# Two feed-forward layers computed as seven block products, with hidden activations passed through DRAM

## The reference

```python
D_MODEL = 1024
D_FF = -(-8 * D_MODEL // (3 * 256)) * 256
def swiglu(xn, w_gate, w_up, w_down):
    h = jax.nn.silu(jnp.einsum('bsd,df->bsf', xn, w_gate)) * jnp.einsum('bsd,df->bsf', xn, w_up)
    return jnp.einsum('bsf,fd->bsd', h, w_down)
...
        hp = hp + swiglu(rms_norm(hp, ln_ffn[layer]), w_gate[layer], w_up[layer], w_down[layer])
        hs = hs + swiglu(rms_norm(hs, ln_ffn[layer]), w_gate[layer], w_up[layer], w_down[layer])
```

## Time and profile before

| | us |
|---|---|
| median of 3 runs | 2554.5 |
| lowest, highest | 2551.43, 2556.82 |
| span of the profiled execution | 2554.3 |
| first feed-forward layer, 889.00 to 1679.65 | 790.65 |
| pooling mixer and the norm behind it, 1679.65 to 1749.30 | 69.65 |
| second feed-forward layer, 1749.30 to 2542.40 | 793.10 |
| tail | 11.90 |

### The profile page before, as it was taken

The page is one execution under the profiler, slowest core; times in us unless marked ns, Lnnn a source line. Parts: engine busy times, 40 slices in busy tenths (PEclk is TensorE's granted clock), DMA queues, the critical chain, the costliest instruction groups (busy, mean ns, idle before and its releaser), DMA issues.

```text
span 2554.3 us, 39454 instructions
## 1 busy us (share of the span) xinstructions
PE 2465.1 (97%) x16305; PEld 2288.4 (90%) x16305; DVE 1059.7 (41%) x2210; ACT 673.8 (26%) x1186; POOL 196.5 (8%) x239
## 2 busy tenths in 40 slices
PE   7999988888889999999999999999999999999998
PEld 6778866555669999999999999999999999999998
DVE  4312056555774633333223333467333333333325
ACT  5221133355673321111101111164201111111112
POOL 0020000045432000000000000040000000000000
PEclk9999999999999999999999999998999999999999
DMA  4321289944562011111011111111111111111101
GB/s 165 111 94 59 114 316 409 364 158 156 181 196 71 17 50 50 50 50 47 20 50 43 40 50 50 35 47 34 50 50 42 42 50 50 50 50 50 34 26 71
DMA packets 119688, 229.42 MB, mean 90 GB/s; under 512 B 6260, under 2 KB 82373, under 8 KB 116972
## 3 DMA queue, kind: packets, MB, share of 16 engines
q1 hardware_dynamic: 113731, 179.60, 20.3%
q0 software_dynamic: 5808, 47.64, 5.4%
HBM read 209.32 MB, written 51.41 MB: 102 GB/s over the span
## 4 chain that ended last, share of the span: by engine, by line
PE 87%; issue 4%; DMA 3%; DVE 3%; SPq 2%; ACT 1%; POOL 1%; DVEq 0%; ACTq 0%
PE ps L1834 74%; PE ps L1868 2%; PE ps L793 2%; DMA kraw<-cache_win_k_a 2%; PE ps L777 2%; PE ps L812 2%; SPq L905 1%; PE ps L1923 1%; DMA wraw<-w_out 1%; PE ps L2151 1%; ACT sm L681 1%; POOL sm L1066 1%; PE ps L1962 1%; SPq L908 0%; PE ps L1937 0%
## 5 line engine op out<-in xcount | busy, mean ns | idle before, releaser
L1834 PE MATMUL ps<-xn,ws 128*128 128x384 f32 (+1 forms) x6744 | 1117.8, 326 | 0.0
L1834 PEld LDWEIGHTS ps<-xn,ws 128*128 128x128 f32 x6744 | 1112.1, 188 | 0.8
L1834 PE MATMUL ps<-hh,ws 128*128 128x384 f32 (+1 forms) x3168 | 530.5, 327 | 0.0
L1834 PEld LDWEIGHTS ps<-hh,ws 128*128 128x128 f32 x3168 | 524.8, 188 | 0.0
L1655 DVE TENSOR_TENSOR act_h<-act_s,ps 128x384 f32<-128x384 f32 x132 | 70.2, 532 | 847.2 <-ACT act_s L1264 847.2
L1264 ACT ACTIVATE act_s<-ps 128x384 f32<-128x384 f32 x132 | 62.5, 473 | 1205.2 <-PE ps L1834 1096.5
L1634 DVE TENSOR_TENSOR x<-ps,x 128x384 f32<-128x384 f32 (+1 forms) x552 | 284.5, 532 | 187.2 <-PE ps L1834 185.4
L1834 PE MATMUL ps<-wp,xn 128*128 128x512 f32 (+1 forms) x1080 | 245.4, 389 | 0.0
L1834 PEld LDWEIGHTS ps<-wp,xn 128*128 128x128 f32 (+1 forms) x1080 | 196.3, 182 | 48.9
L622 DVE TENSOR_TENSOR ws<-wraw,ws 128x2048 fp32r<-128x2048 f32 x63 | 143.8, 2282 | 5.2 <-ACT ws L617 5.2
L1066 POOL TENSOR_TENSOR sm<-sm,pstat 128x128 f32<-128x128 f32 (+7 forms) x96 | 108.7, 1145 | 320.0 <-DVE pstat L554 320.0
(11 more groups left out here) (213 smaller groups left out, 1793.4 us busy)
## 6 DMA issues: line engine op xcount, KB each, us to landing
wraw<-w_gate SPq DMA_DIRECT2D x22, 1024.0 KB, 5.2
wraw<-w_up SPq DMA_DIRECT2D x22, 1024.0 KB, 5.2
wraw<-w_down SPq DMA_DIRECT2D x22, 1024.0 KB, 4.9
kraw<-cache_win_k_a SPq DMA_DIRECT2D x8, 2048.0 KB, 14.7
vraw<-cache_win_v_a SPq DMA_DIRECT2D x8, 2048.0 KB, 11.4
kraw<-cache_k_b SPq DMA_DIRECT2D x64, 256.0 KB, 5.8
vraw<-cache_v_b SPq DMA_DIRECT2D x64, 256.0 KB, 11.5
o_wk_s<-cache_win_k_a POOLq DMA_DIRECT2D x8, 2032.0 KB, 9.6
```

Source lines behind the costliest of these rows:

```text
L1834: r = mm(out, w(a), m(b_), start=(i == 0 and q_ == 0), stop=(i == n - 1 and q_ == 2))
```

## The change

A product of matrices cut into 2 by 2 blocks needs seven block products in place of eight when sums and differences of blocks are multiplied. The changed kernel does this for gate, up and down.

- **Units.** A unit is seven products (`PARTS`) of 272 columns (`BL`, four blocks of tokens, two to a unit: `tp`). 44 units compute gate and up (hidden block, then gate for both `tp`, then up for both), each 7 times 4 times 3 = 84 matmuls. The down product comes after them in pieces (`PIECES`): four pieces of 2 hidden blocks, each 8 units (four groups of output features by two `tp`) of 42 matmuls, and one piece of 3 blocks, 8 units of 63. That is 3696 + 1344 + 504 = 5544 matmuls a layer. Products 4, 5 and 6 of a unit accumulate onto banks of products 0, 2 and 3 once those have been read out.
- **Weights.** Each pair of units (in the last piece each unit) has a weight set, 46 a layer. There is one raw buffer, `wr`. `set_load` waits until the set before is wholly cut; GpSimd makes four sums or differences a set (`set_sum`), ScalarE seven high parts (`set_high`), VectorE seven low parts (`set_low`), each as soon as the product of the same number of the set before is through. On VectorE they stand between the outputs of the unit that ends a set.
- **Activations.** The normed input is kept as seven blocks a slot (four plain or summed ones in `xnr`, three in `x2a`, `x2b`); hidden blocks are formed as seven, high and low, in `stg` (which takes the place of `x`), stored to DRAM (`hidden_store`, 1.95 MB a block and `tp`) and loaded again into eight slots ahead of their piece (`slot_load`: 14 times 272 columns, 1.95 MB). `x` itself goes to DRAM and comes back (`x_kept`, 4.5 MB).
- **Outputs.** ScalarE saves the first product, VectorE makes the rest of the sums from PSUM (`part_out` in gate and up, `down_out` in down), GpSimd makes four differences a hidden block and `tp` and, in the last piece, adds three blocks a unit to `x` (`kept_add`).
- **Around.** Norming is by quarters of 272 columns, seven blocks each; only the first `tp` is ready at the layer's start. Four row blocks are turned in the last four units, five after the layer, in both layers.

The places of new names in the changed code: L1145 to L1163 the loads on SyncE, L1302 `set_sum`, L1917 and L1929 the reciprocal and the norming, L1953 the low part of a normed block, L1958 `set_low`, L2000 to L2012 `part_out`, L2043 to L2059 `down_out`.

SyncE's queue in the down products, before: the loads of three kinds of weights, two slots, each load behind its wait.

The core of the diff:

```diff
+        PARTS = 7
+        PART_BANK = (0, 1, 2, 3, 0, 2, 3)
+        PIECES = ((9, 10), (0, 1), (2, 3), (4, 5), (6, 7, 8))
+        LASTP = 4
+        UNIT_A, UNIT_Z, UNIT_L = 4 * PAIRS, 4 * PAIRS + 8 * LASTP, 4 * PAIRS + 8 * LASTP + 8
+        SETS = UNIT_Z // 2 + 8
+        PHYS = (1, 0, 6, 7, 2, 3, 5, 4, 0, 1, 7, 6, 2, 3, 5, 4, 0, 1, 2, 7, 6, 5)
+        SLOT0 = (0, 4, 8, 12, 16)
+        SLOTS = 22
...
+        def slot_last(n):
+            p, tp, _ = slot_at(n)
+            return UNIT_A + 8 * p + 6 + tp if p < LASTP else UNIT_Z + 4 * tp + 3
+        def slot_free(n):
+            earlier = [m for m in range(n) if PHYS[m] == PHYS[n]]
+            return slot_last(earlier[-1]) if earlier else 42 + PHYS[n] // 4
...
+            def set_load(layer, w):
...
+                    sp.wait_ge(norm_pieces, 16 * norm_block(layer, 1) + 1)
+                else:
+                    sp.wait_ge(set_lo, PARTS * set_number(layer, w))
+                kind, b, dp, _ = ffn_at(set_begin(w))
+                if kind == "down":
+                    n, b0 = len(PIECES[b]), PIECES[b][0]
+                    src = d["w_down"][layer].rearrange("(b h p) n -> p h b n", h=2, p=P)[:, :, b0:b0 + n, dp * 256:dp * 256 + 256]
+                    dst = wr[:, 0:512 * n].rearrange("p (h b n) -> p h b n", h=2, b=n)
+                    for h in range(2):
+                        sp.dma_start(dst[:, h], src[:, h]).then_inc(set_loaded[w % 2], 16)
+                else:
+                    src = d["w_" + kind][layer].rearrange("(k p) n -> p k n", p=P)[:, :, b * 256:b * 256 + 256]
+                    sp.dma_start(wr[:].rearrange("p (k n) -> p k n", k=KD), src).then_inc(set_loaded[w % 2], 16)
...
+            def slot_load(layer, n):
+                p, tp, b = slot_at(n)
+                half, kt = divmod(PHYS[n], 4)
+                sp.wait_ge(part_done, done(layer, slot_free(n), PARTS - 1))
+                sp.wait_ge(hidden_stored[tp], 16 * ((PAIRS - 1) * layer + b + 1))
+                sp.dma_start(xnr[:, 4 * kt:4 * kt + 4, half].rearrange("p q a n -> p q (a n)").bitcast(F32),
+                             hid[b, tp][:, 0:8 * BL].rearrange("p (q n) -> p q n", q=4)).then_inc(slot_loaded[PHYS[n]], 16)
+                sp.dma_start(x2[half][:, kt].rearrange("p q a n -> p (q a n)").bitcast(F32), hid[b, tp][:, 8 * BL:14 * BL]).then_inc(slot_loaded[PHYS[n]], 16)
...
+            def ffn_sp(layer):
+                set_load(layer, 0)
+                set_load(layer, 1)
+                sp.wait_ge(norm_pieces, 16 * norm_block(layer, 1) + 16)
+                sp.dma_start(x_kept[:], x[:]).then_inc(x_stored, 16)
+                for u in range(UNIT_L):
+                    kind, b, _, tp = ffn_at(u)
+                    w = set_at(u)
+                    for n in range(SLOTS):
+                        if n not in KEPT and slot_free(n) == u - 1:
+                            slot_load(layer, n)
+                    if u == set_begin(w) and 1 <= w < SETS - 1:
+                        set_load(layer, w + 1)
+                    if 2 <= u - 1 < UNIT_A - 4 and ffn_at(u - 1)[0] == "up":
...
+            def set_sum(layer, w, q):
+                n = set_number(layer, w)
+                dst = set_cols(w, wcf[:, q, 1]) if q in (3, 5) else set_cols(w, wsum[:, 2 - q])
...
+                elif q == 2:
+                    pool.wait_ge(set_loaded[w % 2], set_loads(layer, w))
+                    if n:
+                        pool.wait_ge(set_lo, PARTS * (n - 1) + 3)
+                if q == 2:
+                    a, b, op = raw_quarter(w, 0, 1), raw_quarter(w, 1, 1), ALU.add
+                elif q == 1:
+                    pool.wait_ge(set_sums, 4 * n + 1)
+                    a, b, op = set_cols(w, wsum[:, 0]), raw_quarter(w, 0, 0), ALU.subtract
+                elif q == 3:
+                    a, b, op = raw_quarter(w, 0, 0), raw_quarter(w, 0, 1), ALU.subtract
+                else:
+                    pool.wait_ge(set_sums, 4 * n + 2)
+                    a, b, op = raw_quarter(w, 1, 0), set_cols(w, wsum[:, 1]), ALU.subtract
...
+            def set_high(layer, w, q):
+                if w:
+                    act.wait_ge(part_done, done(layer, set_end(w - 1), q))
...
+                    act.wait_ge(set_loaded[w % 2], set_loads(layer, w))
+                else:
+                    act.wait_ge(set_sums, 4 * set_number(layer, w) + {2: 1, 1: 2, 3: 3, 5: 4}[q])
+                act.activation(set_cols(w, wc[:, q, 0]), set_source(w, q), ACT.Copy).then_inc(set_hi, 1)
...
+            def set_low(layer, w, q):
+                dve.wait_ge(set_hi, PARTS * set_number(layer, w) + q + 1)
+                tt(set_cols(w, wc[:, q, 1]), set_source(w, q), set_cols(w, wc[:, q, 0]).bitcast(F32), ALU.subtract).then_inc(set_lo, 1)
...
+                        dve.wait_ge(parts_act, by_act(layer, u, "e1"))
+                    tt(kept, src, kept, ALU.add).then_inc(parts_dve, 1)
+                    return
+                if q == 2 and p == 0 and tp == 0 and dp < 2:
+                    dve.wait_ge(x_loaded[0], 16 * (layer + 1))
+                    if dp:
+                        dve.wait_ge(x_loaded[1], 16 * (layer + 1))
+                if q == 3:
+                    dve.wait_ge(parts_dve, by_dve(layer, u, "x22a"))
+                dst = block_of(u, *{2: (1, 1), 3: (1, 1), 4: (0, 0), 5: (0, 1), 6: (1, 0)}[q])
+                tt(dst, src, dst, ALU.add).then_inc(parts_dve, 1)
...
+            def ffn_dve(layer):
+                for u in range(UNIT_L):
+                    kind, p, dp, tp = ffn_at(u)
+                    w = set_at(u)
+                    if u == 0:
+                        chunk_recip(1 + 2 * layer, 2)
+                        norm_quarter(layer, 1, 0, 0)
+                        norm_quarter(layer, 1, 1, 0)
+                    for q in range(PARTS):
...
+                        if u == 0 and q == 2:
+                            norm_quarter(layer, 1, 1, 1)
+                        if u == 0 and q == 3:
+                            norm_differences(layer, 1)
+                        if u == 0 and q == 5:
+                            norm_low(layer, 1, V11)
+                            norm_low(layer, 1, V2)
+                        if u == set_end(w) and w < SETS - 1 and q:
+                            set_low(layer, w + 1, q - 1)
+                        if 0 < u <= UNIT_A and ffn_at(u - 1)[0] == "up" and q >= 3:
+                            for i in ((0, 1), (2, 3), (4, 5), (6,))[q - 3]:
+                                hidden_low(layer, u - 1, i)
+                    if u == set_end(w) and w < SETS - 1:
+                        set_low(layer, w + 1, 6)
...
-            def down(layer, b, par):
-                pe.wait_ge(hidden_lo, b * GU_PER + (FFN_G[layer] + GU_PER))
-                last = b == PAIRS - 1
-                if last:
-                    pe.wait_ge(half_lo, 3 * layer + 3)
-                else:
-                    pe.wait_ge(unit_lo, unit_of(layer, "down", b) + 1)
-                for idx in range(ADD_PER):
-                    kt, c = divmod(idx, NC)
-                    if last:
-                        c, kt = divmod(idx, KD)
...
-                    c0, cn = CH[c]
-                    group(b * ADD_PER + (FFN_A[layer] + idx), idx, cn,
-                          [(lambda a, j=j: ws[2][:, a, j * D + kt * P:j * D + kt * P + P], lambda a, j=j: hh[:, par, j, a, c0:c0 + cn])
-                           for j in range(2)])
...
+            def unit(layer, u):
+                kind, p, dp, tp = ffn_at(u)
+                w = set_at(u)
+                before = u - 1 if u >= UNIT_Z + 4 else u - 2
...
+                if kind == "down" and dp == 0:
+                    for j in range(len(PIECES[p])):
+                        n = slot_of(p, tp, j)
+                        if n in KEPT:
+                            pe.wait_ge(hidden_lo, PARTS * (SLOTS * (layer + 1) + tp - 1))
+                        else:
+                            pe.wait_ge(slot_loaded[PHYS[n]], slot_count(layer, n))
+                for q in range(PARTS):
+                    if u == set_begin(w):
+                        pe.wait_ge(set_lo, PARTS * set_number(layer, w) + q + 1)
+                    if u < 2:
+                        pe.wait_ge(norm_lo, 28 * norm_block(layer, tp) + 4 * (q + 1))
+                    if q < 4:
+                        if before >= 0:
+                            name = first_bank(before, q)
+                            if name == "g11":
+                                pe.wait_ge(parts_act, by_act(layer, before, name))
...
+                        else:
+                            pe.wait_ge(parts_act, by_act(layer, u, "e1" if kind == "down" else "s1"))
+                    elif q == 5:
+                        pe.wait_ge(parts_dve, by_dve(layer, u, "x22a" if kind == "down" else "u4"))
+                    else:
+                        pe.wait_ge(parts_dve, by_dve(layer, u, "x22b" if kind == "down" else "c22"))
```

(5 more changed lines are left out.)

1030 lines of the change are left out of this document (619 added, 411 removed).

## The result

The changed kernel takes 2750.5 us (median of 4 runs, 2745.67 to 2751.56) against 2555.1 for the kernel before in the same comparison: a ratio of 1.076, 95% interval 1.0745 to 1.0776. The profiled execution spans 2743.8 us, 189.5 more than before. The forecast was 2610, with 2515 to 2655 as its range. The direction was right; the size was 55 where 195 was measured, outside the range.

The account below looks back on a forecast made before the run. The prediction took TensorE's matmuls to bound the kernel (97% busy); 159.6 and 13.0 us saved there against added waits, clock, pooling, tail and memory costs summed to +55.4, so 2609.7 us, with a range of 2515 to 2655.

Parts of the forecast that it names:

- Matmuls: Both layers: 11088 matmuls of 272 columns at 0.1267 us replace 9504; -159.6 us, and -13.0 for the rest.
- Rival C: A 272-column matmul costs only 0.1133 to 0.117 us, some 115 us less in all: 2495; chance 0.05.
- Gate and up: Gate and up in full swing: slack of VectorE and DMA covers everything, the set load by 1 us; nothing added.
- Starts: First two units of each layer wait for VectorE's norming, low parts and outputs: +22.2 us each, +44.4.
- Step to down: From gate and up to down, slot loads hold up units 45 and 46: +14.4 us a layer, +28.8.
- piece changes: Three a layer in down: four slot loads ahead of a weight set delay it; +9.8 us each, +58.8.
- Last piece: Last eight down units: one raw buffer makes a load-sum-cut period of 11.5 us against 7.98 of matmuls; +53.6.
- Clock: TensorE at half rate after some four long waits a layer, about 2.5 us each: +20 us, from none to +56.
- Two engines on one memory: VectorE slowed beside GpSimd, counting only in the starts, piece changes and last piece: +6 us, from 0 to 36.
- Rival B: VectorE's two-operand operations stop for the whole of GpSimd's; +40 us in starts, piece changes, last piece: 2650; chance 0.10.
- Rival A: Loads of one queue share the engines, so small set loads land early despite slots: 88 us less, 2521; chance 0.22.
- Rival D: Chains at the starts and in the last piece a third shorter than summed: 33 us less, 2577; chance 0.12.

Follow-up runs that it names:

- sums_small: Changed kernel with GpSimd's four sums of every weight set on 8 columns, cuts reading raw quarters (output not the layer's): 2638.5 us, ratio 1.032.
- store_behind: Changed kernel with only the order of the hidden stores changed, issued behind the set load they stood ahead of: 2704.5 us (one run).
- combo4: combo3 with four of seven VectorE low-part cuts of the first half's hidden block moved one unit later: 2508.9 us, ratio 0.982 to the kernel before.
- combo3_sums: combo3 with GpSimd's four sums of every weight set on 8 columns (output not the layer's): 2487.3 us, ratio 0.974 to the kernel before.
- outs_first: Changed kernel with VectorE's outputs of unit 0's first three products ahead of the second half's reciprocal and scalings: 2753.1 us (one run).
- slots_spread: Changed kernel with each weight set's load issued first and one slot load behind it, instead of four slots ahead: 2651.0 us, ratio 1.037.
- two_raw: Changed kernel with a second raw weight buffer in the last piece, each set loaded one unit earlier: 2692.0 us, ratio 1.053.
- combo3: Changed kernel with spread slot loads, second raw buffer in the last piece and hidden stores behind set loads together: 2537.4 us, ratio 0.994 to the kernel before.
- pool_beside: Kernel before with 400 unused GpSimd multiplications of two SBUF tiles added from about 1752 us on: 2558.8 us against 2555.8.

## Why the prediction was wrong, point by point

1. *Matmuls.* Right, and 13 us too dear: the pitch at 272 columns is 0.1256, where the line through 320 and 384 gave 0.1267. Rival C (0.1133 to 0.117) did not come. The price of a lone matmul by the Trainium skill ("TensorE: Matmul & The Clock Gate", Back-to-back issue gap), 0.1158 as an estimate, would have been 10 ns too low here.

2. *Gate and up.* **The step that failed.** It booked nothing, on a cover that the text itself put at 1 us: the set landing 12.7 us into the pair of units and wanted at 13.7. In the trace it lands at 17.8 to 18.7. Less the store's 4.8 and the load's 4.9 the forecast has the load go out at about 3.0; it goes out at 7.8, since it waits for VectorE's last cut and VectorE is late. The 27 us of VectorE a block did not come out of the text's own prices (52 operations at 0.35 and 0.6 are 22), and 34.8 were measured; 4.7 of these go when the sums are small. Both edges of the cover were off: in sums_small the set lands at 15.3 to 16.8 and costs only 2 to 3.5 us a layer, so it is wanted near 16 and not at 13.7. The cost is 81 us of the 134 by which the sum missed: 53 in units 4k+1, which need the store ahead of the load as a second cause (store_behind), and 28 in units 4k, which either another place for VectorE's cuts (combo4) or smaller sums (combo3_sums) remove. The prediction's last sentence named the item, and the sum gave it no value: a cover of 1 us that rests on 27 us of unproven VectorE prices should have been carried as a bound of its own.

3. *Starts.* The mechanism holds (outs_first), 55 in place of 44. VectorE's operations beside GpSimd took more: four differences of 272 columns took 4.43 us at 917.36, and 1.49 at 887.27 with GpSimd idle.

4. *Step to down*, 5. *piece changes.* The mechanism was right to the instruction, and slots_spread takes the second to zero. The first came to 37 in place of 28.8. In the piece changes the landing came at 24.4 us where 22.6 stood; the rest of the 13.0 to 14.5 against 9.8 a change is 13 matmuls at a pitch of 0.23 after the wait, 1.3 us, and the late cuts that follow.

6. *Last piece.* Mis-sized, a period of 13.8 us or more for 11.5, and 91.5 us in all for 53.6: the second largest miss. The sum ran from the load over GpSimd to the cut and closed there. In the program TensorE's last three products come behind the first cut of the next set, and the next load behind the last cut: 3.9 us of TensorE's work is in the loop, not beside it. two_raw opens it.

7. *Clock.* 598 matmuls at a pitch of 0.19 to 0.3, 60 us above the others in all, where +20 was booked (+56 was its upper bound). The long waits cost less than I took, 1.3 us each; the many short ones in units 0, 1, 45 and 76 to 82 were not counted. They shrink with the waits: 23 us in combo3. This time is in the rows of the units, not beside them.

8. *Pooling and tail.* 23 and 5.4 for 11.7 and 4.7. The row gains stand one behind another as said (6.94 us for three), but the cut of `pool_w` now also falls into this stretch, on ScalarE and VectorE.

9. *Two engines on one memory.* +6 was booked, from 0 to 36. Rival B was set at 0.10 because 0.22 us added was not the 1.65 of four GpSimd operations. That compared the wrong things: each of the four takes 0.41, and VectorE waits for what is left of the one that it meets. Read so, the very row agrees with B.

Rival A had 0.22, on 16 engines with a mean share of 0.13 that could let a small load pass. The queue passes its transfers in turn: the set took 14.1 us behind four slots, 3.5 in front of one. Rival B's mechanism is what happened, though an operation waits for the rest of the other's and not for all of it. Its price of 40 was too low: without the sums the changed kernel is 112 us faster, since B was priced in the starts, the last piece and the piece changes and not where VectorE is busiest. Rival D (0.12), chains a third shorter than summed, went the other way: the starts took 55 for 44.4, the last piece 91.5 for 53.6. That the change makes the kernel slower was forecast for the right reason: the waits of parts 3 to 6 are all there, and by themselves outweigh what the matmuls save.

Open: why the granted clock between the layers stays at 0.50 for some 20 us longer in some executions. It seems to vary from one execution to the next and not with the edit: the four of combo3 took 2532.8 and 2534.0 us with a mean clock of 0.976 and 0.974, and 2540.8 and 2543.6 with 0.970 and 0.969, but only one of them has a trace. A start with less on VectorE was not tried either; with 28 us a layer it is the largest wait left in combo4.

## What to carry to other kernels

A change that takes work off the bounding engine and puts it on three others is judged by its in-order queues: for each load, what stands ahead of it, and for each output that frees a bank, what stands ahead of it, at the unit where that engine is busiest and not on the mean. In a cycle (load, sum, cut, product, cut, load) follow the chain until it closes before giving a period. And where a cover comes out small against the prices that it is worked out from (1 us against 27 here), book a price for its failure: four edits of order and place without a single operation less were worth 242 us here, more than the 173 us of matmuls that the change took away.

## What the runs showed of the hardware

- VectorE's operations on SBUF tiles alone and GpSimd's exclude each other: the one that starts second waits until the other's has ended. VectorE's cuts of 384 columns, 0.55 us alone, took from 0.55 to 0.86 by how much of a 0.46 us GpSimd operation was left, and the latter took 2.39 to 2.42 against a 2.28 us cut. With one operand in PSUM VectorE's operations kept their 0.55 us (pool_beside).
- After a wait of 11 us TensorE runs some 13 matmuls of 272 columns at 0.23 us, at a granted clock of 0.50, before it is back at 0.1256: 3 us at 1.2 GHz. Beside this stands the 14 us at 0.51 behind pooling, where it ran mostly small tiles.
- A 0.5 MB set load lands in 3.5 us with a 1.95 MB load right behind it in the same queue, and in 14.1 with four such loads ahead of it. A 1 MB set load lands in 6.5 us with such a store behind it and in 10.0 to 10.8 with one just ahead.
